# Delta rule's inverse in 32-column blocks, and the attention's bias band stored row by row

## The reference, cut to what matters

```
A = jnp.where(strict, jnp.einsum('bnhid,bnhjd->bnhij', kb, kc) * L, 0.0)
sol = lax.linalg.triangular_solve(A + jnp.eye(C, dtype=A.dtype), rhs, left_side=True, lower=True)
```

```
s = s + band_bias.astype(jnp.float32).reshape(1, 1, HKV, G, W, 2 * W)
```

## Time and profile before

| | |
|---|---|
| median of 3 runs | 3091.36 us (3088.34 to 3091.62) |
| the profiled execution's own time | 3083.48 us |
| its span, first to last instruction | 3081.6 us |
| mean granted share of TensorE's full clock | 0.985 |
| PE busy | 2952.6 us, 96% of the span, 15641 matmuls |
| DVE, ACT, POOL busy | 1743.6, 1217.6, 625.9 us |

### The profile page before, as it was taken

One profiled execution on the slowest core, in us unless ns is written; L12 is line 12 of the kernel. 1 busy time (PEld: TensorE's weight loads), 2 busy tenths in 40 slices (PEclk: granted clock), 3 DMA queues, 4 the chain that ended last, 5 costly groups with the idle time before them and its releaser, 6 DMA issues. The chain is left out here.

```text
span 3081.6 us, 39976 instructions
## 1 busy us (share of the span) xinstructions
PE 2952.6 (96%) x15641; PEld 2324.9 (75%) x15641; DVE 1743.6 (57%) x2362; ACT 1217.6 (40%) x1857; POOL 625.9 (20%) x359
## 2 busy tenths in 40 slices
PE   8998999999999999999899999999999999999997
PEld 6675667788887888777677777777777788877885
DVE  4557766565544223754458767667566433347856
ACT  4344754443333112444543334233444333533333
POOL 1111013334443222420000000000000244421233
PEclk9999999999999999999999999999999999999998
DMA  4221000243335223343421112114323233456643
GB/s 154 94 90 69 8 8 8 95 157 110 110 110 225 89 91 106 128 163 97 123 93 62 49 66 69 53 62 136 112 100 111 95 109 109 165 191 235 232 148 130
DMA packets 145442, 335.97 MB, mean 109 GB/s; under 512 B 12392, under 2 KB 53608, under 8 KB 145128
## 3 DMA queue, kind: packets, MB, share of 16 engines
q1 hardware_dynamic: 118184, 268.65, 25.6%
q10 hardware_dynamic: 27072, 64.76, 5.4%
HBM read 234.80 MB, written 97.52 MB: 108 GB/s over the span
## 5 line engine op out<-in xcount | busy, mean ns | idle before, releaser
L2378 PE MATMUL psum<-normed_hi,w_hi 128*128 128x512 f32 x984 | 422.0, 429 | 8.6 <-ACT buffer L2026 5.2
L2380 PE MATMUL psum<-normed_hi,w_lo 128*128 128x512 f32 x984 | 387.2, 394 | 0.0
L2379 PE MATMUL psum<-normed_lo,w_hi 128*128 128x512 f32 x984 | 386.3, 393 | 0.0
L1536 POOL TENSOR_TENSOR w_lo<-raw,w_hi 128x1024 fp32r<-128x1024 f32 x79 | 198.0, 2506 | 665.5 <-ACT w_hi L1218 617.2
L2378 PEld LDWEIGHTS psum<-normed_hi,w_hi 128*128 128x128 f32 x984 | 186.6, 190 | 57.4 <-issue 20.5
L3775 POOL TENSOR_TENSOR w_lo<-raw,w_hi 128x1024 fp32r<-128x1024 f32 x1 | 3.4, 3447 | 1093.0 <-ACT w_hi L2026 1093.0
L2380 PEld LDWEIGHTS psum<-normed_hi,w_lo 128*128 128x128 f32 x984 | 186.1, 189 | 41.3
L2379 PEld LDWEIGHTS psum<-normed_lo,w_hi 128*128 128x128 f32 x984 | 186.9, 190 | 37.6 <-issue 6.8
L1218 ACT ACTIVATE w_hi<-raw 128x1024 fp32r<-128x1024 f32 x79 | 83.7, 1059 | 292.8 <-PE psum L1098 256.0
L2026 ACT ACTIVATE buffer<-psum,par 128x512 f32<-128x512 f32 (+1 forms) x131 | 93.3, 713 | 260.7 <-PE psum L2380 246.0
L1830 DVE TENSOR_TENSOR res<-psum,res 128x512 f32<-128x512 f32 x80 | 55.2, 691 | 209.8 <-PE psum L1098 209.7
(11 more groups left out here) (572 smaller groups left out, 7445.7 us busy)
## 6 DMA issues: line engine op xcount, KB each, us to landing
raw<-in_w_in SPq DMA_DIRECT2D x75, 512.0 KB, 4.3
scratch_in<-buffer ACTq DMA_DIRECT2D x59, 512.0 KB, 2.7
raw<-in_w_mlp SPq DMA_DIRECT2D x42, 512.0 KB, 3.7
scratch_gate<-gate_out ACTq DMA_DIRECT2D x60, 256.0 KB, 2.0
gate_in<-scratch_gate SPq DMA_DIRECT2D x27, 512.0 KB, 4.2
scratch_hid<-hidden_out ACTq DMA_DIRECT2D x44, 256.0 KB, 4.2
split_plain<-scratch_y SPq DMA_DIRECT2D x20, 512.0 KB, 7.2
raw<-in_w_br SPq DMA_DIRECT2D x18, 512.0 KB, 4.6
```

The costliest lines, as they stand in the source:

```text
L1536: pool.tensor_tensor(to[1].lo, to[0], to[1].hi.bitcast(F32), ALU.subtract).then_inc(w_lo, 1)
L2378: pe.matmul(out, hi, xh, start=k == 0, stop=False)
L2379: pe.matmul(out, hi, xl, start=False, stop=False)
L2380: mm = pe.matmul(out, lo, xh, start=False, stop=k == DC - 1)
```

## The change

`by_halves` becomes `by_blocks`, which takes the size of the diagonal blocks. At levels 2 to 4 all three groups, and at level 1 the second and the third group, are now computed in four blocks of 32 x 32 in four groups of 32 columns. Levels 5 and 6, the first chunk's level 1, and the first group of level 1 stay as they were; the latter writes 64 x 64 blocks, since level 5 of the chunk before left them in the bank. The contraction stays over all 128 rows.

The band's store becomes eight transfers, one for each head's row, at planned times 119, 131, ... 203 in place of 110. Each adds 16 to `row_out`, so the three waits ask for 128.

```diff
             def band():
-                yield T_BAND + 20.0
-                sp.wait_ge(placed, len(ranges))
-                sp.dma_start(d["band"], row[0:8].unsqueeze(1).to_broadcast([8, P, 384])).then_inc(row_out, 16)
+                for h in range(8):
+                    yield T_BAND + 29.0 + 12.0 * h
+                    sp.wait_ge(placed, len(ranges))
+                    sp.dma_start(d["band"][h:h + 1], row[h:h + 1].unsqueeze(1).to_broadcast([1, P, 384])).then_inc(row_out, 16)
                 yield T_AFTER + 4.5
                 sp.wait_ge(o_out, 16 * NB)
-                sp.wait_ge(row_out, 16)
+                sp.wait_ge(row_out, 128)
...
-                        by_halves(first, masked, inv, lvl == 6 or 7 * c + lvl == 1).then_inc(mid_done, 1)
+                        by_blocks(first, masked, inv, P if lvl == 6 or 7 * c + lvl == 1 else P // 2 if lvl in (1, 5) else P // 4).then_inc(mid_done, 1)
...
                         if lvl < 6:
-                            by_halves(second, turned, mid, lvl == 6 or 7 * c + lvl == 1).then_inc(low_done, 1)
+                            by_blocks(second, turned, mid, P if 7 * c + lvl == 1 else P // 2 if lvl == 5 else P // 4).then_inc(low_done, 1)
                         yield at_i[c] + LEVEL * (lvl - 1) + 4.1
-                        by_halves(first, mid, turned, lvl == 6 or 7 * c + lvl == 1).then_inc(up_done, 1)
-
-            def by_halves(to, left, right, whole):
+                        by_blocks(first, mid, turned, P if lvl == 6 or 7 * c + lvl == 1 else P // 2 if lvl == 5 else P // 4).then_inc(up_done, 1)
+
+            def by_blocks(to, left, right, size):
                 for h in range(4):
...
+                    for first in range(0, P, size):
+                        rows = slice(first, first + size)
+                        mm = pe.matmul(to[rows, h * P + first:h * P + first + size], hd(left)[:, h, rows], hd(right)[:, h, rows],
+                                       start=True, stop=True)
                 return mm
```

More of the change, by code:

```diff
@@ L2961, in prepare @@
                 dve.wait_ge(lru_out, 16 * BT)
-                dve.wait_ge(row_out, 16)
+                dve.wait_ge(row_out, 128)
                 dve.memset(state[:, 0], 0.0).then_inc(state_ready, 4)
```

## The result

The changed kernel takes 3063.3 us (median of 3 runs, 3058.9 to 3063.9) against 3091.4: the ratio is 0.9908, with a 95% interval from 0.9886 to 0.9931. That is 28.1 us, 0.9%, faster. The same kernel run once more as an experiment gave 26.0 us. The prediction was 3068, with a gain of 23.5 us. The two profiled spans (3081.6 and 3061.5) lie only 20.2 apart, since the execution profiled before was 7.9 us faster than its median.

A forecast was written before the change was run, and what follows sets the result against it. PE was taken as the bound, busy 96% of the span, with DVE close behind in the delta rule. 13 + 10.5 = 23.5 us off the profiled 3083.5 gave 3060.0, plus 7.9 for the median: 3068 us, range 3057 to 3085.

The forecast's parts named there:

- the likeliest case's own range: Whole kernel, if both parts gain as forecast: 3062 to 3075 us around 3068, chance 0.64.
- The step for 32 columns: Inverse: four column groups side by side, 32 ns a round, 0.21 us saved in each of 86 groups, 18 us.
- What is retained, 13 of 18: Inverse in the delta rule: 13 us of the 18 saved reach the end, since DVE is late next.
- the rise from 5.7 to 10: Delta rule: PE's waits for DVE's mask L3047 go up from 5.7 us, perhaps to 10.
- The band, 10.5: Band's stretch: eight row stores remove PE's hole, priced at 11.5 us, of which 10.5 are gained.
- The 1 us left in: Band: about one us of the 11.5 not counted as gain, as the next `lru` matmuls also wait, 0.94 us.
- the duration of a row's store: Band: one row's store takes 4 us at 51 GB/s, between bounds of 1.7 and 27.5 us.
- The spread over the 128 copies: Band: with one source row the next dimension, 128 copies, sets the spread, over all 16 DMA engines.
- No gain from 32 columns: Rival, inverse: loads or streams of four column groups share what two now use up; 3081 us, chance 0.11.
- The holes swallow it: Rival: PE's saving becomes waits for DVE, `lru` keeps part of the band's hole; 6 and 6 gained, 3079, chance 0.11.
- The start rate decides, 3121: Rival, inverse: records can't follow at under 29 ns in the mean, costing 40 us; 3121 us, chance 0.09.
- One row's store on one engine: Rival, band: 27.5 us a row holds each of eight loads by 12.5, 100 us; 3178 us, chance 0.05.

The follow-up runs named there:

- mid_first: Changed kernel with ACT's copy of `mid` at level 6 planned 1.5 us earlier, ahead of the next chunk's exponential: 3053.5 us, ratio 0.9879 to the kernel before.
- pool_queue: Changed kernel with the band's eight rows in one store, issued by GpSimd on its own queue: 3065.0 us, ratio 0.9915 to the kernel before.
- pairs: Changed kernel with the band stored as four stores of two rows each, at every second of the eight places: 3071.9 us, ratio 0.9934.
- inverse_only: Changed kernel with the band's one store as before, the 32-column blocks kept: 3072.8 us, ratio 0.9943 to the kernel before.
- band_only: Changed kernel with the inverse in halves as before, the band's eight row stores kept: 3077.0 us, ratio 0.9955 to the kernel before.
- blocks_outer: Changed kernel with its two loops exchanged, so the four heads of one block follow each other: 3101.1 us, ratio 1.0037 to the kernel before.

## Why the prediction was right, and where its steps were off

The time was right: 3063.3 for 3068, within the likeliest case's own range. The two terms were 13 and 10.5 us; the two stages gave 13.7 and 11.6.

**The step for 32 columns: right.** The sum had 32 ns for four records, a group of 0.50 us and a double one of 0.75; the trace has 0.46 and 0.76, rounds of 32 ns in the single group, and a half of a double group in 0.30 for the 0.25 of the sum. The busy time of the groups fell by 18.5 us for 18. The 64-column step in proportion to its width was the observation that carried this, and the four records in flight within 15 ns are its confirmation. The rule of the Trainium skill that spoke against it (TensorE: Matmul & The Clock Gate, Part 1, never less than about 25 ns from start to start) doesn't hold for these records: 32 of them in 0.30 us are 9 ns apart. Its Part 3, some 4 ns between tiles in different column groups, comes near: the least distances here are 6 to 7 ns. What the prediction did not see is a condition: it spoke of four column groups "side by side", as a property of the place in the array. The exchanged loops showed that it is also one of the program's order, and that it was worth 36 us here. The order that the change uses was the right one, but the prediction gave no reason for it; that part was luck.

**What is retained, 13 of 18: the number right, the reason not.** The sum let 5 us go into waits for DVE. In the delta rule's stretch, from the same gemm matmul to the same one (440.0 us before, 426.3 after), PE's busy time fell by 16.0 us (413.8 to 397.8) and its holes grew by 2.3 (26.2 to 28.5). The holes first. The idle time before the groups at levels 1 to 5 grew by just these 2.3 us (6.8 to 9.1): the part that ACT's copy ends by 1.4, the part that DVE's mask ends by 0.9. The weight loads' waits for the mask, all sizes together, are 9.6 us for 8.2 (5.7 of the halves and 2.5 of the whole products), not the rise from 5.7 to 10 foretold. The 11.1 us ahead of level 6 stood there before, 9.7 of them ended by ACT's copy, and mid_first took them out with DVE's work unchanged. DVE does end holes of its own, the longest single one (3.7 us, at 1724.5) among them, but these are as long as before. So what was to be had next was ACT's fixed order at level 6.

Then the busy time: 16.0 for the 18.5 of the groups. Here the granted clock comes in, for which the sum had no term. In this stretch it falls to half for 3.4 us at a time, three times in the changed kernel:

```profile
1653.70:1657.10 3.40, 3.36 (x15) 3.36 (x16) 1.31 (x3) 1.54 (x2) 0.00 (x0) 0.50 0.37 146
1728.80:1732.20 3.40, 3.40 (x16) 3.21 (x16) 1.89 (x4) 0.00 (x0) 0.00 (x0) 0.50 0.00 0
1950.60:1954.00 3.40, 3.40 (x13) 2.82 (x12) 3.24 (x6) 0.12 (x1) 0.00 (x0) 0.51 0.00 0
```

In the kernel before it does so twice:

```profile
1665.50:1668.90 3.40, 3.40 (x40) 3.17 (x40) 1.74 (x3) 0.51 (x2) 0.00 (x0) 0.51 0.12 49
1740.60:1744.00 3.40, 3.38 (x16) 3.40 (x17) 1.80 (x3) 0.00 (x0) 0.00 (x0) 0.50 0.00 0
```

Each stands right behind one of the same three holes of PE (2.1, 3.7 and 2.5 us long in both kernels), but not every such hole is followed by one. At half clock 3.4 us hold the work of 1.7 (an estimate from the two levels). So the third costs the changed kernel 1.7 of the 2.5 us, and 0.8 stay unassigned. The other traces bear it out: the changed kernel's repetition also has three (and gains 13.8 there), pool_queue three (14.0), pairs two (15.5), inverse_only one (17.0), and band_only, whose PE program in the stretch is that of before, has 10.2 us at half clock in place of 6.8 and is 1.3 longer. Put at the clock of the kernel before, the five kernels with the blocks gain 15.3 to 15.7 us. That 13 met 13.7 is thus partly luck: the waits took less than the prediction gave them, and the clock took some of the rest.

**The band, 10.5: the mechanism right, the size within 1 to 1.5 us.** The hole, the half clock behind it and the second wait before the `lru` matmuls were one chain from one transfer, and all went: 11.6 us, 11.9 and 12.0 in three traces. The 1 us left in for the next `lru` matmuls was too much: their wait is still there (0.97 us for 0.94), but it stands in both kernels and so in no difference. The step that failed inside it is the duration of a row's store: "4 us, since the same bytes leave a narrow source at 51 GB/s". It lands after 9.5 to 17.0 us and moves at 27 GB/s. The spread over the 128 copies came as foretold; the pace did not carry over from eight source rows to one. It cost nothing: the load behind the first row landed after 10.3 us, inside the 17.5 that ACT left it, and behind the row of 17.0 us nothing urgent stood. With two rows a store the `lru` load met a store of 17 us, and there one stall came back, as pairs shows. That an issue costs SP at most 0.82 us was off as well (0.59 in the median, up to 4.7), without an effect on the time that a trace shows.

**The rivals.** No gain from 32 columns: refuted by 0.46 for 0.69 us. The holes swallow it: refuted by 13.7 to 17 us retained, and by 11.6 for the 6 of the band. The start rate decides, 3121: refuted by 9 ns against its 15 ns threshold. The order of blocks_outer, though, gives 0.90 us a group, near the 0.93 of that rival, but with starts 5 to 6 ns apart among them, so through another mechanism. One row's store on one engine: refuted by 13.7 engines.

## What to carry to other kernels

Small products in column groups of the array were worth their extra instructions here only with neighbours in program order in different column groups; write the loop so and read the length of one whole group, not the mean of one matmul, which was 199 ns in the good and in the bad order. A store with few source rows should be judged by how long it lasts against the slack of the loads that meet it: split it until it is shorter than that slack, or let the urgent loads go ahead of it. Another queue alone is no cure that these runs show. And after a gain on the bound engine look at which of its waits are queue order on another engine, for these may be had by one planned time. Before two gains of a few us are compared, count in both traces how long the granted clock was at half: here that explained 3.3 us that looked like an effect of the code.

## What the runs showed of the hardware that was not expected

- The order of the records decides the overlap of column groups. Four heads of one block in succession: 0.90 us a group; blocks alternating: 0.46. For 64 columns in the exchanged order 31 groups took 26.8 us in place of 19.5. The starts show that PE passes up to three waiting records to reach free columns.
- One source row broadcast 128 times moves at 27 GB/s although 13.7 DMA engines work on it (0.78 us a packet of 1.5 KB), two rows at 23 GB/s on 1.9 engines (0.12 us a packet), eight rows at 51 GB/s on 7.2 (0.215). With more engines on a row the packets grow longer. What limits a single row no run separates.
- The Trainium skill (DMA: Bandwidth & Descriptors, section Why a DMA increments its semaphore by 16 and not by 1) has the slowest dimension over 1 set the number of engines. The traces agree in all three cases: 2 rows 1.9, 8 rows 7.2, 1 row (128 copies next) 13.7 of 16.
- A slow store holds back transfers issued during it, on its own queue for nearly its whole length (a load of 34.8 us in inverse_only) and on other queues too: ACT's store, 2.6 us in the median, took 20.4 us in the kernel before and 23.6 in pool_queue, with the engines busy for 45 to 47%.
- After the same hole of PE (3.7 us ahead of L2457 in the changed kernel, L2456 before) the granted clock fell to half for 3.4 us in the changed kernel and the kernel before, for 6.8 us in band_only and not at all in inverse_only. The hole alone doesn't say what it will cost.
